# Weighted values of two attention heads issued together, in a two-layer diffusion backbone on Trainium2

## What is computed

```python
def attend(q, k, v):
    s = jnp.einsum('bqhd,bkhd->bhqk', q, k).astype(jnp.float32) * MLA_SCALE
    p = jax.nn.softmax(s, axis=-1).astype(v.dtype)
    return jnp.einsum('bhqk,bkhd->bqhd', p, v)
```

## Time and profile before

| | |
|---|---|
| median of 3 runs | 1514.2 us (1510.49 to 1516.42) |
| the profiled execution | 1513.88 us, its span 1512.1 us |
| PE busy | 1416.6 us, 94% |
| DVE busy | 794.8 us, 53% |
| ACT busy | 521.1 us, 34% |
| POOL busy | 218.3 us, 14% |
| mean granted TensorE clock | 0.978 |
| DMA | 210.52 MB, mean 139 GB/s |

### The profile page before, as it was taken

One profiled execution on the slowest core, in us unless ns is written; L12 is line 12 of the kernel. 1 busy time (PEld: TensorE's weight loads), 2 busy tenths in 40 slices (PEclk: granted clock), 3 DMA queues, 4 the chain that ended last, 5 costly groups with the idle time before them and its releaser, 6 DMA issues.

```text
span 1512.1 us, 19509 instructions
## 1 busy us (share of the span) xinstructions
PE 1416.6 (94%) x8034; PEld 1131.5 (75%) x8034; DVE 794.8 (53%) x1106; ACT 521.1 (34%) x787; POOL 218.3 (14%) x203
## 2 busy tenths in 40 slices
PE   2899999999999999799999999978999899899996
PEld 0365766777877787477777777757868899799996
DVE  3575557433554464643322443346776576776664
ACT  3242245233222131433212332113444453464451
POOL 4300100060301134200000000220003201500012
PEclk9999999999999999899999999997999999999998
DMA  8322220444542125244444445322314463456552
GB/s 329 159 93 74 98 70 1 153 167 167 195 168 70 56 84 181 77 160 153 167 145 148 167 141 180 140 98 84 126 56 150 161 248 125 155 167 195 196 194 71
DMA packets 56584, 210.52 MB, mean 139 GB/s; under 512 B 6213, under 2 KB 7365, under 8 KB 55600
## 3 DMA queue, kind: packets, MB, share of 16 engines
q1 hardware_dynamic: 54176, 194.22, 37.3%
q0 software_dynamic: 2320, 15.05, 2.6%
HBM read 205.58 MB, written 3.67 MB: 138 GB/s over the span
## 4 chain that ended last, share of the span: by engine, by line
PE 87%; DVE 7%; DMA 2%; ACT 2%; POOL 1%; issue 1%; SPq 0%; DVEq 0%; POOLq 0%; ACTq 0%
PE ps L1229 25%; PE ps L1230 24%; PE ps L1231 24%; PE ps L1258 3%; PE ps L1437 2%; PE ps L1462 2%; DVE normed L865 2%; PE ps L1528 1%; PE ps L1538 1%; DMA raw<-in_units 1%; PE ps L1449 1%; DVE wl L813 1%; DVE rstd L858 1%; DVE xl L874 1%; PE ps L1329 1%
## 5 line engine op out<-in xcount | busy, mean ns | idle before, releaser
L1229 PE MATMUL ps<-xh,wh 128*128 128x512 f32 (+2 forms) x1376 | 475.6, 346 | 33.1 <-DVE xl L874 28.8
L813 DVE TENSOR_TENSOR wl<-raw,wh 128x1024 fp32r<-128x1024 f32 x272 | 359.3, 1323 | 251.1 <-ACT wh L590 247.9
L1230 PE MATMUL ps<-xl,wh 128*128 128x512 f32 (+2 forms) x1376 | 467.0, 339 | 0.0
L1231 PE MATMUL ps<-xh,wl 128*128 128x512 f32 (+2 forms) x1376 | 466.1, 339 | 0.0
L590 ACT ACTIVATE wh<-raw 128x1024 fp32r<-128x1024 f32 x272 | 287.0, 1055 | 320.4 <-PE ps L1231 315.7
L1229 PEld LDWEIGHTS ps<-xh,wh 128*128 128x128 f32 (+1 forms) x1376 | 261.3, 190 | 80.0 <-issue 40.3
L1231 PEld LDWEIGHTS ps<-xh,wl 128*128 128x128 f32 (+1 forms) x1376 | 261.9, 190 | 30.6
L1230 PEld LDWEIGHTS ps<-xl,wh 128*128 128x128 f32 (+1 forms) x1376 | 262.2, 191 | 29.1 <-issue 1.0
L1229 PE MATMUL ps<-hid_h,wh 128*128 128x512 f32 (+1 forms) x512 | 172.0, 336 | 0.0
L1230 PE MATMUL ps<-hid_l,wh 128*128 128x512 f32 (+1 forms) x512 | 170.6, 333 | 0.0
L1231 PE MATMUL ps<-hid_h,wl 128*128 128x512 f32 (+1 forms) x512 | 170.3, 333 | 0.0
(11 more groups left out here) (204 smaller groups left out, 1478.1 us busy)
## 6 DMA issues: line engine op xcount, KB each, us to landing
raw<-in_units SPq DMA_DIRECT2D x272, 512.0 KB, 3.3
mod_ring<-in_mod_units SPq DMA_DIRECT2D x80, 512.0 KB, 4.0
first_ring<-in_mod_units SPq DMA_DIRECT2D x16, 512.0 KB, 9.1
filters<-filt POOLq DMA_DIRECT2D x2, 1280.0 KB, 6.2
filt<-filters POOLq DMA_DIRECT2D x2, 1280.0 KB, 10.9
ftab<-in_fwd POOLq DMA_DIRECT2D x3, 768.0 KB, 5.3
h<-in_x POOLq DMA_DIRECT2D x1, 2048.0 KB, 18.2
counts<-in_counts POOLq DMA_DIRECT2D x2, 1024.0 KB, 5.3
```

The lines of the kernel that those rows point to most:

```text
L813: dve.tensor_tensor(wl[:, g % SLOTS, :], raw[:, g % SLOTS, :], wh[:, g % SLOTS, :].bitcast(F), ALU.subtract)\
L1229: pe.matmul(dst, w_h, m_h, start=first, stop=False)
L1230: pe.matmul(dst, w_h, m_l, start=False, stop=False)
L1231: return pe.matmul(dst, w_l, m_h, start=False, stop=last)
```

## The change

- PE no longer multiplies each job's probabilities with its values a job later. It does so for two heads (an even and the next odd one, a pair) in one go, after the transposes of the job that follows the pair. In it, the products of the two heads alternate block of keys by block of keys, one on partitions 0 to 63 and the other on 64 to 127.
- `probs_t` becomes three buffers that the jobs take in turn; the third, `probs_t2`, lies behind `v_t`.
- ACT copies both banks of a full job (two copies); DVE copies none, and its wait for the transposes goes. `pt_act` counts copies instead of jobs (`copies(jb)`). `pv_done` counts pairs instead of jobs.
- DVE makes the outputs of a pair one job later than before: outputs(jb - 2).

```diff
--- before.py
+++ after.py
@@ -270,12 +270,14 @@
         with ExitStack() as s:
             sig = alloc(s, "sig", (KB, T))
             probs = alloc(s, "probs", (4, T))
-            probs_t = alloc(s, "probs_t", (2, 4, SEQ))
+            probs_t01 = alloc(s, "probs_t", (2, 4, SEQ))
             fh_of = by_layer(s, "fh", 4, (0, SHIFT))
             fl_of = by_layer(s, "fl", 4, (0, SHIFT))
             q_t = alloc(s, "q_t", (HEADS, T))
             k_t = alloc(s, "k_t", (HEADS, T))
             v_t = alloc(s, "v_t", (T // 128, HEADS * VH))
+            probs_t2 = alloc(s, "probs_t2", (4, SEQ))
+            probs_t = [probs_t01[:, 0, :, :], probs_t01[:, 1, :, :], probs_t2]
             roped = sq[:, :, :].rearrange("p a (b t) -> p a b t", t=SEQ)
         with ExitStack() as s:
             alloc(s, "pad_c", (16 * KBYTE,))
@@ -722,10 +724,11 @@
                     if jb + 1 < len(jobs):
                         exponentials(jb + 1)
                     act.wait_ge(transposed[layer], jb + 1)
-                    if jb >= 2:
-                        act.wait_ge(pv_done[layer], jb - 1)
-                    act.activation(probs_t[:, jb % 2, 0:2, :], ps[:, 6, :].rearrange("p (k q) -> p k q", q=SEQ),
-                                   ACT.Copy).then_inc(pt_act[layer], 1)
+                    if jb >= 3:
+                        act.wait_ge(pv_done[layer], (jb - 1) // 2)
+                    for half in range(2 if jobs[jb][1] == 0 else 1):
+                        act.activation(probs_t[jb % 3][:, 2 * half:2 * half + 2, :],
+                                       ps[:, 6 + half, :].rearrange("p (k q) -> p k q", q=SEQ), ACT.Copy).then_inc(pt_act[layer], 1)
                 for _ in straight(layer, "wo"):
                     pass
                 for j, p in straight(layer, "pool"):
@@ -1043,8 +1046,8 @@
 
                     hd, s = jobs[jb]
                     if hd % 2:
-                        dve.wait_ge(pv_done[layer], jb + 1)
                         pair = jb // 2
+                        dve.wait_ge(pv_done[layer], pair + 1)
                         src = ps[:, pair % 2, 0:SEQ]
                         t = slice(s * SEQ, (s + 1) * SEQ)
                         chained(dve.tensor_copy(fh_of[layer][:, hd // 2, t], src))
@@ -1055,19 +1058,14 @@
                 maxima(1)
                 normalise(0)
                 for jb in range(len(jobs)):
-                    if jobs[jb][1] == 0:
-                        dve.wait_ge(transposed[layer], jb + 1)
-                        if jb >= 2:
-                            dve.wait_ge(pv_done[layer], jb - 1)
-                        dve.tensor_copy(probs_t[:, jb % 2, 2:4, :], ps[:, 7, :].rearrange("p (k q) -> p k q", q=SEQ))\
-                           .then_inc(pt_dve[layer], 1)
                     if jb + 1 < len(jobs):
                         normalise(jb + 1)
                     if jb + 2 < len(jobs):
                         maxima(jb + 2)
-                    if jb:
-                        outputs(jb - 1)
-                outputs(len(jobs) - 1)
+                    if jb >= 2:
+                        outputs(jb - 2)
+                for jb in range(len(jobs) - 2, len(jobs)):
+                    outputs(jb)
 
                 def branch_out(name, b):
 
@@ -1441,27 +1439,31 @@
                     keys = T if jobs[jb][1] == 0 else CTX
                     pe.wait_ge(probs_ready[layer], 2 * jb + 2)
                     if jb:
-                        pe.wait_ge(pt_act[layer], jb)
-                        pe.wait_ge(pt_dve[layer], min(jb, HEADS))
+                        pe.wait_ge(pt_act[layer], copies(jb))
                     for kb in range(keys // 128):
                         for qb in range(2):
                             at = (kb % 2) * SEQ + qb * 128
                             mm = pe.transpose(ps[:, 6 + kb // 2, at:at + 128], probs[:, 2 * (jb % 2) + qb, kb * 128:(kb + 1) * 128], ident)
                     mm.then_inc(transposed[layer], 1)
 
-                def weighted_values(jb):
+                def weighted_values(pair):
+
+                    jb = 2 * pair + 1
                     hd, s = jobs[jb]
                     tb0, nb = (0, 4) if s == 0 else (2, 2)
-                    pair = jb // 2
-                    if hd % 2 == 0 and pair >= 2:
+                    if pair >= 2:
                         pe.wait_ge(o_ready[layer], pair - 1)
-                    pe.wait_ge(pt_act[layer], jb + 1)
-                    pe.wait_ge(pt_dve[layer], min(jb + 1, HEADS))
-                    rows = slice(64 * (hd % 2), 64 * (hd % 2) + 64)
+                    pe.wait_ge(pt_act[layer], copies(jb + 1))
                     for kb in range(nb):
-                        mm = pe.matmul(ps[rows, pair % 2, 0:SEQ], v_t[:, tb0 + kb, hd * VH:(hd + 1) * VH],
-                                       probs_t[:, jb % 2, kb, :], start=kb == 0, stop=kb == nb - 1)
+                        for half in range(2):
+                            mm = pe.matmul(ps[64 * half:64 * half + 64, pair % 2, 0:SEQ],
+                                           v_t[:, tb0 + kb, (hd - 1 + half) * VH:(hd + half) * VH],
+                                           probs_t[(jb - 1 + half) % 3][:, kb, :], start=kb == 0, stop=kb == nb - 1)
                     mm.then_inc(pv_done[layer], 1)
+
+                def copies(jb):
+
+                    return 2 * min(jb, HEADS) + max(jb - HEADS, 0)
 
                 pe.wait_ge(q_ready[layer], 1)
                 if ns == 2:
@@ -1476,9 +1478,9 @@
                     if jb + 2 < len(jobs):
                         scores(jb + 2)
                     transposes(jb)
-                    if jb:
-                        weighted_values(jb - 1)
-                weighted_values(len(jobs) - 1)
+                    if jb >= 2 and jb % 2 == 0:
+                        weighted_values(jb // 2 - 1)
+                weighted_values(len(jobs) // 2 - 1)
 
                 def branch_out(name, ready, before):
                     mh, ml = (mixh_of[layer], mixl_of[layer]) if name == "hy_out" else (fh_of[layer], fl_of[layer])
```

## The result

| | before | after |
|---|---|---|
| median | 1515.01 us (4 runs, 1510.49 to 1516.42) | 1502.42 us (4 runs, 1500.22 to 1504.69) |
| the profiled execution | 1513.88 us, span 1512.1 | 1501.06 us, span 1499.3 |
| attention of layer 0 | 57.31 us | 49.34 us |
| attention of layer 1 | 36.89 us | 32.21 us |
| the rest of the span | 1417.9 us | 1417.7 us |

The account below looks back on a forecast made before the run. PE was taken to bound full jobs, with a softmax loop close behind in short ones. Layer 0's 7.7 and layer 1's 4.1 us give 11.8: profiled execution 1513.9 to 1502.1, median 1502.4 us, range 1498 to 1508.5.

Parts of the forecast that it names:

- A pair costs one head's price: Weighted values: both heads' matmuls run beside each other, so a full pair takes 1.87 us, not 3.74.
- one support: End of layer 1 before: 16 matmuls on 64-column halves overlap, ending after 2.86 us instead of 3.7.
- ScalarE has room, PE still bounds the full jobs: Full jobs, both copies on ScalarE: PE needs 3.73 us per job, ScalarE 2.65, VectorE 2.62.
- Layer 0's full half: Full jobs of layer 0: 4 x 1.87 = 7.5 us saved, less 2 x 0.4 of stalls, gives 6.7.
- Stalls from the copies: PE waits for copies: 0.4 us before jobs 6 and 8 of layer 0, 1.4 before job 6 of layer 1.
- The softmax loop in the short half: Layer 0's short jobs: the loop of normalise, maxima and exponentials holds each job to 2.3 us.
- The 0.6 us for the second copy of job 7: Layer 0: that copy stands ahead of job 9's exponentials in ScalarE's queue, costing about 0.6 us.
- The short half: Short jobs of layer 0: 1.7 us saved, less about 0.6 for job 7's second copy, gives 1.0.
- Third buffer, semaphores, nil: Waits for buffers, banks 0 and 1 and later outputs in both attentions: price nil.
- The turns: Rival at weighted values: the halves take turns, a pair costs 3.74 us, total 3.5 us slower, 1517.7; chance 0.05.
- The clock: Rival: PE's holes of up to 1.4 us, or earlier `wo`, cost the gain; 1510 to 1525 us, chance 0.02.

Follow-up runs that it names:

- second trace of the change: The changed kernel traced again with no edit: attentions 49.34 and 32.21 us, ratio to the kernel before 0.9915.
- the run on one half: Changed kernel with both heads of a pair accumulated on partitions 0 to 63: attentions 58.18 and 39.05 us, ratio to before 1.0031.
- head after head: Changed kernel with a pair's products issued one head after the other instead of alternating by blocks: attentions 53.01 and 35.84 us.
- copies alone: Kernel before with only both copies moved to ScalarE, weighted values still head by head: attentions 57.04 and 36.61 us, ratio 1.0000.
- maxima first: Changed kernel with VectorE's maxima(jb + 2) put ahead of normalise(jb + 1): attentions 48.09 and 32.21 us.
- two buffers: Changed kernel with two buffers of transposed probabilities instead of three, ScalarE's wait to match: attentions 50.92 and 35.17 us.
- copies shared: Changed kernel with VectorE again copying each full job's second bank, with its wait: attentions 52.19 and 35.67 us, ratio to before 0.9957.
- two jobs later: Changed kernel with a fourth buffer of transposed probabilities, weighted values and outputs one more job later: attentions 49.97 and 31.35 us.

## Why the prediction was right

Forecast 11.8 us less, 7.7 and 4.1 in the two layers; measured in the traces 12.65, 7.97 and 4.68, with the rest of the span equal to 0.2 us. The mechanism held, and the sum is 0.9 us short. Two things about the total are luck: the rest of the span is 1414.6 us in the second trace of the change, 3 us less, so its being equal here is chance; and the kernel before has its median at 1515.0 with the fourth run, 0.8 above the 1514.2 from which the forecast was counted, which makes good what the sum lacks.

- *A pair costs one head's price.* 1.95 us (1.88 from start to start) for 1.87. Right, and the run on one half shows it to be the whole gain. The rule of the Trainium skill, "TensorE: Matmul & The Clock Gate", section "The mechanism", that weight loads overlap running matmuls only when the row groups differ, is contradicted by the change itself: its two halves use the same 128 rows, and 1.22 us of loads lie in 1.87 us of matmuls without a gap.
- *But one support was wrong.* I put the incomplete overlap at the end of layer 1 before (2.86 us) down to the second head's copies. With all copies long done, "head after head" takes the same 2.86, so the order of issue is enough to explain it. (Copies can hold the second head back too, if they end later: 3.19 us in "copies alone".) The estimate held only because the change issues block by block, which I had not seen to matter; head after head, 7.3 of the 12.65 us would have been missing.
- *ScalarE has room, PE still bounds the full jobs.* Right: from one full pair's weighted values to the next is 7.26 us (224.78 to 232.04) for 7.45. Scores that follow transposes directly take 1.72 to the next transposes, not 1.82, and they start 0.88 and 0.95 us after those transposes, where weighted values started after 0.97 and 1.03. Together with an earlier end of normalise before job 1 (1.72 us from the scores before it to its transposes, 1.93 in the kernel before) this makes 0.5 of the 0.6 us by which layer 1 was underestimated. Layer 0's full half, up to job 8's transposes, gave 7.2 us for 6.7, for the same reasons.
- *Stalls from the copies.* Right in place and size: 0.40 us twice where 0.4 was forecast, 1.26 before job 6 of layer 1 for 1.4; from the last transposes to `wo` 4.23 for 4.2 us. Two terms in it were off and nearly cancel: a pair of copies takes 1.09 instead of 1.20, and its signal 0.14 instead of 0.05.
- *The softmax loop in the short half.* 2.30 us between reciprocals for 2.3; "maxima first" confirms the cause. The 0.6 us for the second copy of job 7 are there too: the maxima of job 9 are done at 243.32 us, and its exponentials start at 243.93, when ScalarE's copies end. The short half gave 0.8 us for 1.0.
- *Third buffer, semaphores, nil.* The price was right, but the buffer itself carries 1.5 us per layer.
- *The turns, 3.5 us slower.* They didn't occur. Made real on one half: 3.0 in the attentions, total 1.0031.
- *The clock.* I gave it 0.02. It did not fall in the change, in either trace, but it fell in three variants with one more or one longer hole.

## What to carry to other kernels

Products that need only half of the array's columns ran beside each other here at the price of one, when they alternated in program order; issued one chain of eight after the other they overlapped only in part. Before counting on such a gain, sum the other engines per job and look for loops among them: here the shortened PE uncovered a loop of VectorE and ScalarE and the copies, which took back a third, and reordering two steps and delaying one returned 4 us.
Compare stretches, not totals, where a stretch repeats to 0.01 us and the total scatters by 15.

## What was not expected of the hardware

- The overlap depends on the order of issue with a reach of about four matmuls: 16 matmuls in 1.95 us alternating, 2.86 one head after the other, 3.67 on one half; 8 in 1.08 alternating and 1.09 one head after the other.
- Two copies of 128x512 from PSUM in a row on ScalarE take 1.09 us, where one takes 0.60.
- The clock fell to 1.2 GHz after three holes of 1.27, 1.34 and 1.27 us in PE's work in a row ("two buffers", granted 0.54 after them), after one of 1.77 ("copies shared", 0.52) and in one of 1.64 us ("two jobs later", 0.50), at a price of 1.3 to 1.6 us each time. Two of 1.26 and 1.27 us did not bring it down, in two traces of the change, nor did 1.36, 0.62 and 0.78 us in a row (the change, layer 0) or one of 1.39 us ("two jobs later", layer 1). Where the limit lies was not tried.
